# The low part of a tile made one tile behind its addition, at two boundaries of a two-layer transformer kernel

## The reference, cut to what matters

```
y = concat([y_a, y_b, y_c, y_d]) @ w_out      # first boundary; y = (gelu(gate) * val) @ ffn_down at the second
x = x + rms_norm(y, post_norm)                # post_mix_norm; post_ffn_norm at the second
h = rms_norm(x, pre_norm)                     # pre_ffn_norm; ffn1_norm at the second
hid = h @ up                                  # ffn_up; ffn1_w_gate and ffn1_w_up at the second
rms_norm(t, w) = t * rsqrt(mean(t * t) + 1e-6) * w
```

## Time and profile before

| | |
|---|---|
| median of 3 runs | 3405.69 us (3405.47 to 3410.08) |
| profiled execution, device time | 3409.16 us |
| its span in the trace | 3407.3 us |
| busy: PE, DVE, ACT, POOL | 99%, 66%, 51%, 16% |
| first boundary: first addition, start of body 1 | 440.10 us, 462.48 us |
| second boundary: first addition, start of body 1 | 1192.34 us, 1214.10 us |

### The profile page before, as it was taken

The page is one execution under the profiler, slowest core; times in us unless marked ns, Lnnn a source line. Parts: engine busy times, 40 slices in busy tenths (PEclk is TensorE's granted clock), DMA queues, the critical chain, the costliest instruction groups (busy, mean ns, idle before and its releaser), DMA issues.

```text
span 3407.3 us, 59138 instructions
## 1 busy us (share of the span) xinstructions
PE 3380.9 (99%) x19590; PEld 2953.4 (87%) x19590; DVE 2250.2 (66%) x2934; ACT 1746.8 (51%) x2591; POOL 541.1 (16%) x508
## 2 busy tenths in 40 slices
PE   9999999999999999999999999999999999999999
PEld 7898888888888888888888888888888888888888
DVE  7868687777754475555555599856687656556544
ACT  5445565555544455445444455544566544444433
POOL 1204111111100011111100056611100111111000
PEclk9999999999999999999999999999999999999999
DMA  6524545555566645555566655554556555555665
GB/s 210 161 94 147 189 152 185 190 190 186 188 187 190 189 157 187 185 191 189 186 184 191 215 173 177 181 167 157 171 192 196 188 188 186 187 192 186 185 192 171
DMA packets 175601, 616.16 MB, mean 181 GB/s; under 512 B 20864, under 2 KB 21408, under 8 KB 175136
## 3 DMA queue, kind: packets, MB, share of 16 engines
q1 hardware_dynamic: 175088, 609.84, 55.7%
q10 hardware_dynamic: 432, 5.24, 0.4%
HBM read 610.81 MB, written 4.19 MB: 180 GB/s over the span
## 4 chain that ended last, share of the span: by engine, by line
PE 95%; DVE 2%; issue 1%; ACT 1%; DMA 0%; POOL 0%; DVEq 0%; SPq 0%; POOLq 0%; ACTq 0%
PE acc L393 60%; PE acc L396 30%; DVE weights_low L279 1%; PE acc L408 1%; PE ps_scale L603 1%; PE ps_narrow L2297 0%; PE ps_wide L2273 0%; ACT weights_high L272 0%; PE acc L411 0%; DVE halves_memory L494 0%; PE ps_wide L1380 0%; PE ps_wide L1426 0%; PE ps_wide L1390 0%; PE ps_wide L1384 0%; DMA weights_raw<-in_w_diff_branch 0%
## 5 line engine op out<-in xcount | busy, mean ns | idle before, releaser
L393 PE MATMUL acc<-moving_halves,weights_high 128*128 128x512 f32 x6400 | 2039.6, 399 | 1.8 <-DVE x_T L2566 1.8
L279 DVE TENSOR_TENSOR weights_low<-weights_raw,weights_high 128x1024 fp32r<-128x1024 f32 (+2 forms) x1184 | 1450.0, 1237 | 738.0 <-ACT weights_high L272 736.7
L272 ACT ACTIVATE weights_high<-weights_raw 128x1024 fp32r<-128x1024 f32 (+2 forms) x1184 | 1220.6, 1032 | 797.5 <-PE acc L396 771.6
L396 PEld LDWEIGHTS acc<-moving_halves,weights_low 128*128 128x128 f32 x6400 | 1204.1, 188 | 284.2
L396 PE MATMUL acc<-moving_halves,weights_low 128*128 128x256 f32 x6400 | 1259.3, 278 | 0.0
L393 PEld LDWEIGHTS acc<-moving_halves,weights_high 128*128 128x128 f32 x6400 | 980.3, 189 | 13.3 <-issue 9.8
L393 PE MATMUL acc<-gated_halves,weights_high 128*128 128x512 f32 x2024 | 635.6, 395 | 0.0
L488 ACT ACTIVATE cross_products<-acc 128x256 f32<-128x256 f32 x509 | 194.6, 382 | 693.8 <-PE acc L396 693.7
L396 PEld LDWEIGHTS acc<-gated_halves,weights_low 128*128 128x128 f32 x2024 | 380.2, 188 | 89.9
L511 POOL TENSOR_TENSOR stage_scratch<-unscaled,token_scale 128x256 f32<-128x256 f32 x264 | 217.9, 826 | 1302.6 <-DVE unscaled L494 778.2
L396 PE MATMUL acc<-gated_halves,weights_low 128*128 128x256 f32 x2024 | 397.6, 278 | 0.0
(11 more groups left out here) (361 smaller groups left out, 1972.3 us busy)
## 6 DMA issues: line engine op xcount, KB each, us to landing
weights_raw<-in_w_in SPq DMA_DIRECT2D x271, 512.0 KB, 4.0
weights_raw<-in_ffn_up SPq DMA_DIRECT2D x176, 512.0 KB, 4.3
weights_raw<-in_ffn_w_gate SPq DMA_DIRECT2D x176, 512.0 KB, 4.1
weights_raw<-in_ffn_w_up SPq DMA_DIRECT2D x176, 512.0 KB, 4.6
weights_raw<-in_ffn_w_down SPq DMA_DIRECT2D x160, 512.0 KB, 3.9
weights_raw<-in_ffn_down SPq DMA_DIRECT2D x80, 512.0 KB, 4.2
weights_raw<-in_w_out SPq DMA_DIRECT2D x64, 512.0 KB, 3.8
weights_raw<-in_ffn_w_down SPq DMA_DIRECT2D x32, 256.0 KB, 2.7
```

The source lines that it names most:

```text
L272: core.nc.scalar.activation(core.high[:, slot, k0:nk, :].rearrange("p a b -> p (a b)"), core.raw[:, slot, k0 * P:nk * P], ACT.Copy).then_i ...
L279: core.nc.vector.tensor_tensor(core.low[:, slot, k0:nk, :].rearrange("p a b -> p (a b)"), core.raw[:, slot, k0 * P:nk * P], core.high[:, s ...
L393: core.nc.tensor.matmul(acc[:, t % 2, :, :], core.high[:, u % SLOTS, k, :], parts[:, prod.first[t] + k0 + k, :, :], start=(k0 + k == 0), s ...
L396: core.last = core.nc.tensor.matmul(acc[:, t % 2, 0, :], core.low[:, u % SLOTS, k, :], parts[:, prod.first[t] + k0 + k, 0, :], start=False ...
```

## The change

One constant in the loop of Normed.dve. The low part of tile k - 1 is made after the scaling of y's tile k, instead of that of tile k - 2; the loop has 17 rounds instead of 18. The instructions are the same in number and kind, and the waits too; the additions of tiles 0 and 1 have no low part before them in the kernel before, and now only that of tile 0 has none.

```diff
@@ -748,7 +748,7 @@
             self.held.low_second(dve)
             self.y_scale.refine(dve)
             self.y_scale.ready(dve)
-            BEHIND = 2
+            BEHIND = 1
             for k in range(KT + BEHIND):
                 if k < KT:
                     core.nc.vector.scalar_tensor_tensor(self.y(k), self.y(k), core.v(self.y_gain, k), core.rs[:, :],
```

## The result

The changed kernel takes **3413.76 us** (median of 15 runs, 3413.47 to 3415.27) against 3406.64 us for the kernel before (15 runs, 3405.47 to 3410.08): 7.1 us more, ratio 1.002, 95% interval 1.0013 to 1.0027. The profiled execution of the changed kernel took 3413.73 us.

The account below looks back on a forecast made before the run. PE, busy 99% of the span, was taken as the bound, so DVE costs only where PE waits. Body 1's delays of 2.35 + 2.97 = 5.3 us on the median 3405.69 gave 3411.0 us, range 3408.5 to 3415.5.

Parts of the forecast that it names:

- within: Whole kernel: the measured time differs from the kernel before by no more than about 0.2% (6.8 us); chance 0.74.
- slower: Whole kernel: the measured time is over 0.2% above the kernel before; chance 0.25.
- the forecast's own 4.4 to 6.5: Both boundaries: a period of 1.36 to 1.43 us between additions, costing 4.4 to 6.5 us in total; chance 0.71.
- The wait in the loop: DVE's loop: each low part waits 0.26 us for ACT's high part; period of additions from 1.127 to 1.391 us.
- The last tile: DVE, first boundary: addition 15 comes at 460.97 instead of 456.75, 4.2 us later.
- What PE sees: PE's sums wait for squares from tile 7 on; sum 15 is 2.19 us late, 2.80 at the second boundary.
- Behind the loop: After addition 15, DVE's take of output tile 0 decides; body 1 starts 2.35 and 2.97 us later at the boundaries.
- The rest: Outside the boundary loops: chunk 8's later load costs nothing, and nothing behind body 1 makes up for lateness.
- PE's present starts: PE's sum times in the old order's profile, sum 15 at 460.19 and 1211.82, from which lateness was counted.
- PE hides it: Boundaries: sums stay in time, period under 1.245 and 1.205 us; no cost, 3405.7 us; chance 0.07.
- The handover costs more: ACT to DVE in the loop: period of 1.44 us or more, total 6.8 us or more; chance 0.18.
- The clock falls in the gaps: PE stays at 1.2 GHz after the first quarter, 13.5 us a boundary; 3419 or 3433 us; chance 0.04.

Follow-up runs that it names:

- the full-clock kernel: Against the kernel before: 10 matmuls on constants in PE's stall before each boundary's first sum, still two tiles behind; 3406.07 us against 3407.56, ratio 0.9997.
- the kernel with three behind: Against the kernel before: low parts made three tiles behind instead of two, at both boundaries; 3409.40 us, ratio 1.0007.

## Why the prediction was right

The predicted 3411.0 us was 2.8 under the measured 3413.76, within the range of 3408.5 to 3415.5 (0.95 of it is the median of before, 3406.64 by 15 runs instead of 3405.69 by three, and 1.8 is the cost of the change); the way was right, and the ratio of 1.002 lies at the 0.2% bound that the text set between "within" and "slower", so neither of these two chances is borne out against the other. The two shortfalls point the same way, so nothing cancelled by luck. But the total of 7.1 us lies outside the forecast's own 4.4 to 6.5; the time is inside the range because the range also allowed for a costlier handover and for spread, and neither of these is the reason for the difference that the runs show.

1. *The wait in the loop*: right. Period 1.397 us where 1.391 was predicted, idle 0.18 before the low parts; 1.70 when the handover was made 0.32 longer, 1.13 when the wait was taken away by order alone. The one handover at the end of the old loop was a true sample of the 30 in the new loops.
2. *The last tile*: addition 15 at 20.96 us after addition 0, predicted 20.87.
3. *What PE sees*: right. The squares hold PE, not the low parts; sum 15 came at 22.28 us after addition 0 (462.55 - 440.27), as predicted (462.38 - 440.10). The stalls begin lightly at tiles 7 and 10, and show as idle at 11, 13 and 15.
4. *Behind the loop*: the take decides, as predicted; the cross copy that it waits for was in time, since L494 has no idle before it. PE began 0.13 us after the take ended (465.04 to 465.17), where 0.06 was put. With the 0.09 of step 2 this makes D 24.90 instead of 24.73: 0.18 us short at each boundary, 0.35 in all.
5. *The rest*: nothing else moved. Where DVE fixes D, the time lies as far above the full-clock kernel as the two D do, and from body 1 of the first boundary to addition 0 of the second it is 729.86 us before and 729.96 after.

Of the signs that were named, two came out otherwise in size. L603's wait for L718 went up by 2.0 us and not by 4 or more, because most of the new stalls are booked to the weight load ahead of the sum (0.68 us on PEld where PE's row has 0.26 at tiles 13 and 15). L646's waits went up by 6.4 us, from 1.7 to 8.1, where 5.7 was named: the wait before each last low part also grew, from 0.18 to 0.58 us, since DVE comes to it without the scaling between.

**The term that was mis-sized** is the one subtracted: "PE's present starts". I took them from one execution, in which the clock came back 7.3 us after addition 0 at the first boundary, and called the lag that this gave PE a property of the kernel. The medians say that both D of before are together about 42.14 + 0.57 = 42.7 us in a typical run, not 44.14. This is an estimate, as no trace of a median run was taken, and the other groups' medians of before would make it 42.6 to 43.6. With 42.7 it is 1.4 of the 1.8 us between the predicted 5.3 and the measured 7.1, and the 0.35 us of steps 2 and 4 is the rest. The kernel before had given a sign of it: its profiled execution was 3.5 us above the median of three (2.5 above that of 15), and the prediction subtracted this from the time but not from PE's starts. The new order has less scatter: its 15 runs lie within 1.8 us, the 15 of before within 4.6.

*The rivals.* "PE hides it" fell: PE had no lag to hide 1.397. "The handover costs more" fell in its mechanism (the period is 1.397, under its 1.44), though the total came out near its point of decision, for the other reason. "The clock falls in the gaps" fell. PEclk in the stretches of the changed kernel with the new gaps:

```profile
448.00:456.00 8.00, 7.93 (x43) 6.57 (x41) 6.91 (x19) 4.61 (x12) 0.00 (x0) 1.00 0.00 1
456.00:466.00 10.00, 8.96 (x45) 6.72 (x44) 7.85 (x17) 7.27 (x15) 0.00 (x0) 1.00 0.03 4
1210.00:1221.00 11.00, 9.87 (x48) 7.41 (x47) 8.75 (x18) 7.79 (x17) 0.00 (x0) 1.00 0.03 7
```

PE is busy for 8.96 of 10 and 9.87 of 11 us in the two last stretches, in several short stalls, and the clock is at 2.4 GHz throughout. The section "A second HAM failure mode: psum-queue depth-cycling" of the Trainium skill's page "TensorE: Matmul & The Clock Gate" describes small idle times that make the clock swing; gaps of up to 0.5 us on PE's row, this few, didn't do it here in any of the kernels.

## What to carry to other kernels

When two engines hand tiles to each other in a loop, write down when each product is ready after its input's start, and where its consumer stands in the other engine's order: here 0.995 us against a place at 0.73, and 0.26 us is paid in every round, because the next input stands behind the waiting instruction. How many tiles behind matters less than what stands between: the same distance of one tile cost 7 us or nothing, by whether the low part stood before or behind the next addition. And when an edit turns a bound of one engine into a bound of another, subtract a typical value of the old bound and not that of one profile; several boundaries and runs of related kernels give it.

## What was not expected of the hardware

- The granted clock came back between 4.9 and 8.9 us after addition 0 at boundaries of which the instructions before are the same. It costs the old order about 0.5 us for each us, and the new one nothing.
- It can fall when the stall is over and PE is at work again. At the first boundary of the kernel with three behind, the first sum starts 1.4 us after addition 0, the clock is 1.00 until 442.0 us (addition 0 stands at 440.00) and 0.50 from 442.2 to 448.8, with PE busy for 5.82 of these 6.6 us.
- The clock can drop for a wait in one execution and stay in the next. At the wait of about 1.8 us that PE has in the mixing stage, the windows behind it, in the kernel before and in the changed one, read:

```profile
2188.00:2192.00 4.00, 4.00 (x16) 3.41 (x15) 0.38 (x1) 0.00 (x0) 3.92 (x4) 0.57 0.74 246
```

```profile
2194.00:2198.00 4.00, 4.00 (x25) 3.50 (x24) 0.69 (x2) 1.42 (x2) 3.92 (x4) 1.00 0.72 252
```

  0.57 against 1.00, 16 matmuls against 25 in 4 us. The last weight load of L2678, ahead of the wait, comes 6.0 us later in the changed kernel, and the first of L2273, behind it, 5.0 us later: the dip cost the profiled execution of the kernel before 1 us, and is most of the 1.3 us by which the two profiles come closer behind the boundaries (body 1 of the second is 5.94 us apart, the spans 4.6). From there to the end it is 2193.2 us in the kernel before and 2191.4 to 2192.2 in the other twelve traces.
- A matmul of 256 columns on plain float32 took 0.43 us (20 in 8.6 us, each recorded twice), where two of the same width on the rounded parts (fp32r) take 0.24 us together (465.52 to 465.76 above).
